# First stage of a two-block kernel: other buffers, PSUM temporaries, another order of the products, keys turned on GpSimd

## What is computed

```python
h = x @ w_in                      # 512 columns for S5, then q, k, v, gate
y_s5 = rms_norm(s5_mixer(u, ...)) # complex diagonal state space, 32 groups, 64 states
q, k = rotary(q), rotary(k)       # 4 heads, 64 wide
out = intra + cross               # retention in chunks, decayed state
out = (out - mu) * rsqrt(var + eps) * gn_gain
y = concat([y_s5, out * silu(gate)]) @ w_out
```

## Time and profile before

| | us |
|---|---|
| median of 3 runs (lowest, highest) | 3410.55 (3409.85, 3413.95) |
| profiled execution, its span | 3408.32, 3406.2 |
| PE busy, share of the span | 3110.5, 91% |
| VectorE, ScalarE, GpSimd busy | 1263.8, 880.2, 990.4 |
| first stage, up to the start of "x1" | 399 |

### The profile page before, as it was taken

How to read it: one execution, slowest core, us unless ns; L and a number is a source line. 1 busy time by engine, 2 the same in 40 slices (tenths; PEclk the granted TensorE clock), 3 DMA queues, 4 the chain that set the end, 5 groups by cost and what they waited for, 6 DMA issues and landing times.

```text
span 3406.2 us, 35503 instructions
## 1 busy us (share of the span) xinstructions
PE 3110.5 (91%) x14706; PEld 2549.1 (75%) x14706; DVE 1263.8 (37%) x2407; ACT 880.2 (26%) x1265; POOL 990.4 (29%) x450
## 2 busy tenths in 40 slices
PE   8688899999999979878997887899999999999995
PEld 7566688888888866656776776788887788888884
DVE  7937751221211254464454444302213311111115
ACT  3212232122121133333334444212111411111111
POOL 5301145232233251101332222122222633333332
PEclk9789999999999989988999999899999999999998
DMA  7323212111111111101110000212112111111111
GB/s 179 81 66 114 105 50 62 50 44 62 50 44 56 48 59 63 37 32 32 38 41 35 32 29 28 81 50 73 46 50 99 49 51 60 46 50 50 50 31 50
DMA packets 67392, 193.18 MB, mean 57 GB/s; under 512 B 10304, under 2 KB 18896, under 8 KB 67216
## 3 DMA queue, kind: packets, MB, share of 16 engines
q1 hardware_dynamic: 67232, 190.91, 18.0%
HBM read 165.46 MB, written 25.43 MB: 56 GB/s over the span
## 4 chain that ended last, share of the span: by engine, by line
PE 79%; DVE 10%; ACT 4%; issue 3%; POOL 3%; DMA 1%; SPq 0%; POOLq 0%; DVEq 0%; ACTq 0%
PE PS L365 45%; PE PS L398 7%; PE PS L399 7%; PE PS L400 7%; PE PS L622 3%; PE PS L862 2%; PE PS L751 1%; POOL WL L2134 1%; DVE s L1423 1%; DVE M L1423 1%; PE PS L481 1%; PE PS L421 1%; POOL DD L2260 1%; PE PS L662 1%; PE PS L779 1%
## 5 line engine op out<-in xcount | busy, mean ns | idle before, releaser
L2134 POOL TENSOR_TENSOR WL<-WR,WH 128x1024 fp32r<-128x1024 f32 x241 | 576.6, 2399 | 2167.7 <-ACT WH L960 2167.6
L365 PE MATMUL PS<-XH,WH 128*128 128x512 f32 x2176 | 692.2, 400 | 11.7 <-DVE XL L1462 9.0
L365 PE MATMUL PS<-XL,WH 128*128 128x512 f32 x2176 | 678.9, 393 | 0.0
L365 PE MATMUL PS<-XH,WL 128*128 128x512 f32 x2176 | 675.3, 392 | 0.0
L365 PEld LDWEIGHTS PS<-XH,WH 128*128 128x128 f32 x2176 | 405.5, 191 | 100.5 <-issue 17.8
L365 PEld LDWEIGHTS PS<-XL,WH 128*128 128x128 f32 x2176 | 414.4, 190 | 88.5
L365 PEld LDWEIGHTS PS<-XH,WL 128*128 128x128 f32 x2176 | 412.7, 190 | 88.1
L960 ACT ACTIVATE WH<-WR 128x1024 fp32r<-128x1024 f32 x241 | 253.1, 1055 | 790.2 <-PE PS L400 481.7
L398 PE MATMUL PS<-WH,HH 128*128 128x512 f32 x864 | 338.9, 392 | 14.4 <-POOL HL L2166 14.4
L399 PE MATMUL PS<-WL,HH 128*128 128x512 f32 x864 | 338.1, 391 | 0.0
L400 PE MATMUL PS<-WH,HL 128*128 128x512 f32 x864 | 337.8, 391 | 0.0
(11 more groups left out here) (314 smaller groups left out, 3820.8 us busy)
## 6 DMA issues: line engine op xcount, KB each, us to landing
WR<-in_weights SPq DMA_DIRECT2D x241, 512.0 KB, 3.6
spill<-STQ SPq DMA_DIRECT2D x24, 256.0 KB, 2.0
BR<-brbuf SPq DMA_DIRECT2D x12, 512.0 KB, 4.4
RAWX<-in_xT SPq DMA_DIRECT2D x8, 512.0 KB, 7.1
RES<-in_x SPq DMA_DIRECT2D x8, 512.0 KB, 6.8
xbuf<-XF SPq DMA_DIRECT2D x8, 512.0 KB, 2.7
brbuf<-STG SPq DMA_DIRECT2D x8, 512.0 KB, 2.7
RES<-xbuf SPq DMA_DIRECT2D x8, 512.0 KB, 7.3
```

The lines of the kernel that those rows point to most:

```text
L365: last = e.matmul(PS[:, u.b + h, :], w, x[:, k, 512 * h:512 * h + 512], start=k == 0 and w is w1 and x is xh, stop=k == nk - 1 and w is w2)
L2134: e.tensor_tensor(WL[:, v % NSPL, :], WR[:, v % NRAW, :], WH[:, v % NSPL, :].bitcast(F), ALU.subtract).then_inc(w_lo, 1)
```

## The change

It puts the retention's buffers elsewhere and issues its first loads at the fourth `s_ss`; holds two PSUM banks ("prep") for temporaries and copies in `dve_in`, until the ET table is done; calls for the sines one product earlier; orders kernels, injections, v steps and outputs anew; turns the keys on GpSimd; applies the norm on ScalarE and the gain where the output is cut (C_GN, a column table, takes the place of GNG); and counts `done` without gaps. The new semaphore `r_st` says that the statistics are ready. `pool_keys(i)` has the seven products of `keys(i)` on GpSimd, with its waits.

```diff
--- before.py
+++ after.py
@@ Units.through @@
-        self.done += 1
+        while self.done in self.gone:
+            self.done += 1
 
 
@@ tiles (QKC to YR were 172 to 203, GNG is gone) @@
+        QKC = sb("QKC", 148, [128, 2, 512])
+        KQT = sb("KQT", 152, [128, 2, 4, 128])
+        QX = sb("QX", 156, [128, 2, 2, 128])
+        PT = sb("PT", 158, [128, 2, 4, 128])
+        TA = [sb("TA0", 162, [128, 8, 32]), sb("TA1", 221.25, [128, 8, 32])]
+        KZ = [sb(f"KZ{k}", at, [128, 256]) for k, at in enumerate((202, 203, 163))]
+        YR = sb("YR", 198, [128, 2, 512])
+        VVC = sb("VVC", 164, [128, 3, 512])
+        GGC = sb("GGC", 170, [128, 2, 512])
...
@@ tiles @@
-        KTS = [sb("KTS0", 198, [16, 8, 128]), sb("KTS1", 142, [16, 8, 128])]
+        KTS = [sb("KTS0", 198, [16, 8, 128]), sb("KTS1", 208, [16, 8, 128])]
-        GL = sb("GL", 148, [128, 4, 1024], R)
-        SG = sb("SG", 164, [128, 2, 1024])
+        GL = sb("GL", 182, [128, 4, 1024], R)
+        SG = sb("SG", 174, [128, 2, 1024])
@@ pe_mixer, at its start @@
+            prep = claim(e, "prep", 2, hold=True, told=False)
@@ pe_mixer @@
             values = pe_token_steps(e, "v", "w_in", 1024, 0, 8, XH, XL, range(8))
+            bk.let(prep)
             kernel_of(0)
             inject(0)
             inject(1)
             kernel_of(1)
+            inject(2)
+            inject(3)
+            kernel_of(2)
             tick(values, 1)
-            kernel_of(2)
             kernel_of(3)
-            for q in range(2, 8, 2):
-                inject(q)
-                inject(q + 1)
-                if q < 6:
-                    tick(values, 1)
-            for q in range(4):
-                outputs(q)
-                if q < 3:
-                    tick(values, 1)
+            inject(4)
+            inject(5)
+            tick(values, 1)
+            inject(6)
+            inject(7)
+            tick(values, 1)
+            outputs(0)
+            outputs(1)
+            tick(values, 1)
+            outputs(2)
+            tick(values, 1)
+            outputs(3)
@@ act_in @@
-                if p == 2:
+                if p == 1:
@@ act_s5, kernel_of @@
-                elif p:
-                    e.wait_ge(s_et, 1)
@@ act_retention @@
             for n in range(12):
+                if 3 <= n < 11:
+                    i = n - 3
+                    u = lots["ro", i]
+                    e.wait_ge(r_st, i + 1)
+                    if i >= 2:
+                        e.wait_ge(lots["rt", i - 2].full, lots["rt", i - 2].nfull)
+                    for h in range(4):
+                        c = slice(128 * h, 128 * h + 128)
+                        t = e.activation(YR[:, i % 2, c], PS[:, u.b, c], ACT.Identity, bias=s6[:, 44 + h:45 + h],
+                                         scale=s6[:, 36 + h:37 + h])
+                    t.then_inc(u.drained, 1)
...
-                    e.activation(XH[:, 4:8, 128 * i:128 * i + 128], four(u), ACT.Copy).then_inc(r_hi, 1)
+                    for j in range(4):
+                        t = e.activation(XH[:, 4 + j, 128 * i:128 * i + 128], PS[:, u.b, 128 * j:128 * j + 128], ACT.Copy,
+                                         scale=cols[:, C_GN + j:C_GN + j + 1])
+                    t.then_inc(r_hi, 1)
                 if n == 0:
-                    act_spill(e, "v", 6)
-                    act_spill(e, "v", 7)
+                    for i in (5, 6, 7):
+                        act_spill(e, "v", i)
@@ dve_in @@
+            prep = lots["prep"]
+            near = PS[:, prep.b, 0:256].rearrange("p (a b c) -> p a b c", a=2, b=8)
+            turn = PS[:, prep.b, 256:288]
+            far = PS[:, prep.b + 1, :]
+            e.tensor_copy(near, PP[:, :, 0:8, :]).then_inc(dve, cv.up())
...
             def pw(ri, gg):
-                return PP[:, ri, 0:8, gg].rearrange("p t (g o) -> p g t o", o=1).to_broadcast([128, 4, 8, 16])
+                return near[:, ri, :, gg].rearrange("p t (g o) -> p g t o", o=1).to_broadcast([128, 4, 8, 16])
...
+            m1, m2 = far.rearrange("p (g c) -> p g c", g=4), M2[:, :, :]
                 then(e.tensor_tensor, split(m1), wide(bR), pw(0, gg), ALU.mult)
-                then(e.tensor_tensor, split(m2), wide(bI), pw(1, gg), ALU.mult)
+                e.tensor_tensor(split(m2), wide(bI), pw(1, gg), ALU.mult).then_inc(dve, cv.up())
                 then(e.tensor_tensor, BB[:, gg, 0, :], m1, m2, ALU.subtract)
                 then(e.tensor_tensor, split(m1), wide(bI), pw(0, gg), ALU.mult)
-                then(e.tensor_tensor, split(m2), wide(bR), pw(1, gg), ALU.mult)
+                e.tensor_tensor(split(m2), wide(bR), pw(1, gg), ALU.mult).then_inc(dve, cv.up())
                 e.wait_ge(dve, cv.n)
                 e.tensor_tensor(BB[:, gg, 1, :], m1, m2, ALU.add).then_inc(s_bb, 1)
...
-                v1, v2 = (x.rearrange("p a b -> p (a b)")[:, 0:gn * m].rearrange("p (g c) -> p g c", c=m)
-                          for x in (E1[:, :, :], E2[:, :, :]))
+                v1 = far[:, 0:gn * m].rearrange("p (g c) -> p g c", c=m)
+                v2 = E1[:, :, :].rearrange("p a b -> p (a b)")[:, 0:gn * m].rearrange("p (g c) -> p g c", c=m)
+                then(e.tensor_copy, turn, LL[:, 8:10, :].rearrange("p a b -> p (a b)"))
                 for g in range(0, 16, gn):
-                    bm = lambda x: x[:, g:g + gn].rearrange("p (g o) -> p g o", o=1).to_broadcast([128, gn, m])
-                    cmul(ET[:, g:g + gn, 0, m:2 * m], ET[:, g:g + gn, 1, m:2 * m], ET[:, g:g + gn, 0, 0:m],
-                         ET[:, g:g + gn, 1, 0:m], bm(P1), bm(P0), v1, v2)
+                    bm = lambda k: turn[:, 16 * k + g:16 * k + g + gn].rearrange("p (g o) -> p g o", o=1).to_broadcast([128, gn, m])
+                    aR, aI = ET[:, g:g + gn, 0, 0:m], ET[:, g:g + gn, 1, 0:m]
+                    then(e.tensor_tensor, v1, aR, bm(1), ALU.mult)
+                    e.tensor_tensor(v2, aI, bm(0), ALU.mult).then_inc(dve, cv.up())
+                    then(e.tensor_tensor, ET[:, g:g + gn, 0, m:2 * m], v1, v2, ALU.subtract)
+                    then(e.tensor_tensor, v1, aR, bm(0), ALU.mult)
+                    e.tensor_tensor(v2, aI, bm(1), ALU.mult).then_inc(dve, cv.up())
+                    then(e.tensor_tensor, ET[:, g:g + gn, 1, m:2 * m], v1, v2, ALU.add)
                 m *= 2
                 if m < 128:
                     squared()
             e.wait_ge(dve, cv.n)
             e.tensor_copy(LAM[:, :], LL[:, 7, :]).then_inc(s_et, 1)
+            e.tensor_copy(E2[:, 0, 0:1], far[:, 0:1]).then_inc(prep.drained, 1)
@@ dve_retention, norm, and its order of work @@
-                if i >= 2:
-                    e.wait_ge(lots["rt", i - 2].full, lots["rt", i - 2].nfull)
-                for h in range(4):
-                    c = slice(128 * h, 128 * h + 128)
-                    t = e.scalar_tensor_tensor(YR[:, d, c], PS[:, u.b, c], s6[:, 24 + 2 * h:25 + 2 * h], GNG[:, c],
-                                               ALU.subtract, ALU.mult)
-                    t.then_inc(u.drained, 1) if h == 3 else t.then_inc(dve, cv.up())
+                e.scalar_tensor_tensor(s6[:, 44:48], s6[:, 24:32:2], -1.0, s6[:, 36:40], ALU.mult, ALU.mult).then_inc(r_st, 1)
+
+            def gated(i):
+                d, u = i % 2, lots["ro", i]
-                for h in range(4):
-                    c = slice(128 * h, 128 * h + 128)
-                    t = e.scalar_tensor_tensor(YR[:, d, c], YR[:, d, c], s6[:, 36 + h:37 + h], GGC[:, d, c], ALU.mult, ALU.mult)
-                    t.then_inc(r_y, 1) if h == 3 else t.then_inc(dve, cv.up())
+                e.tensor_tensor(YR[:, d, :], YR[:, d, :], GGC[:, d, :], ALU.mult).then_inc(r_y, 1)
...
-                if n < 8:
-                    keys(n)
+                if 3 <= n < 11:
+                    gated(n - 3)
-                    e.tensor_tensor(XL[:, 4:8, 128 * i:128 * i + 128], four(u), XH[:, 4:8, 128 * i:128 * i + 128].bitcast(F),
-                                    ALU.subtract).then_inc(u.drained, 1)
+                    for j in range(4):
+                        w = slice(128 * i, 128 * i + 128)
+                        t = e.scalar_tensor_tensor(XL[:, 4 + j, w], PS[:, u.b, 128 * j:128 * j + 128], cols[:, C_GN + j:C_GN + j + 1],
+                                                   XH[:, 4 + j, w].bitcast(F), ALU.mult, ALU.subtract)
+                    t.then_inc(u.drained, 1)
@@ gpsimd: pool_keys, new (the seven products of keys(i) as before, on GpSimd), and its call @@
+        def pool_keys(e, i):
...
+            e.wait_ge(qk_in[i % 2], 16 * (i // 2 + 1))
...
+            if i >= 3:
+                e.wait_ge(lots["kv", i - 3].full, lots["kv", i - 3].nfull)
...
-            pool_cut(e, lots["v", 7].units)
+            for i in range(8):
+                if i == 2:
+                    pool_cut(e, lots["v", 7].units)
+                pool_keys(e, i)
@@ sp_s5 and sp_retention @@
             load(e, lots["qk", 7].units)
```

(36 more changed lines are left out.)

71 lines of the change are left out of this document (32 added, 39 removed).

## The result

The changed kernel takes 3432.32 us (median of 4 runs, 3431.33 to 3433.58), the kernel before, run beside it, 3411.65 (3409.85 to 3413.95). The ratio is 1.006, with a 95% interval from 1.0043 to 1.0078: 20.7 us slower. The forecast was 3396, in a range from 3374 to 3411. The profiled execution has a span of 3429.5 us against 3406.2; squares(3) ends at 422.8 instead of 399.4, and that is the whole difference, 23.4 us in these two executions: behind it the traces run alike.

What follows compares the result with a forecast made beforehand. It took VectorE's chain from sines to first turned injection as the bound; first flip at 221 plus retention 164 ends at 385 instead of 399.4, so 3408.3 - 14.4 = 3393.9, or 3396 against the median; range 3374 to 3411 us.

Steps and rivals of the forecast that it cites:

- the head to T: Preparation up to T, the end of ET: T at 119 us instead of 144.0, within 103 to 130.
- one with an input in PSUM does not take turns: Preparation: VectorE operations with a PSUM input run unhindered beside GpSimd; BB's operations 0.72 us each, ending at 71.7.
- Rival D: BB and ET: PSUM does not lift turn-taking, T at 136 to 141; 3419 us from T = 137; chance 0.08.
- from T to the first flip: Stretch from the end of ET to the retention's start: 102.2 us, first flip at 221 instead of 240.9.
- the first output then takes 15.1 us, the others 8.4: Outputs behind PE's stand for T8: only the first runs at PEclk 0.50; with two v steps 52 us.
- the retention: First flip to the end of squares(3): 164 us against 158.5 before, ends 152 and 172.
- Rival C: Retention: GpSimd's rotations and VectorE's norms take turns every step, 172 us or more; 3404 to 3413 us; chance 0.17.
- With one v step moved in, 124: Retention: PE's products alone take 118 us, 124 with the moved v step.
- n = 5, stall 10: Retention, outs(3) waiting for the ro bank, low parts and norm(2): PE stalls 10 us instead of 6.4.
- n = 6 to 8, "3 us, as 3.2 before": Retention, steps 6 to 8: PE stands 3 us, as 3.2 before.
- The mended counter takes the idle 10.05 away: Retention's tail: ScalarE's idle 10.05 us at 364 goes; only 3 us of the tail go, 11 instead of 14.
- Low clock 5: Retention: 5 us added to the sum of 164 for PE's low clock.

Runs made afterwards that it cites:

- e12: Changed kernel with the temporaries of the state-space preparation back in SBUF, orders and waits as changed; 3451.6 us.
- e6: e2 plus, in SyncE's queue, the YP loads behind the first turn's weight loads and the load of QKC's chunk 2 ahead of them; 3417.3 us.
- e2: Changed kernel with one value step moved back ahead of the first output; 3425.7 us.
- e3: Changed kernel with ScalarE's four scaled copies that drain the ro bank issued ahead of the sigmoid of the turn before; 3424.7 us.
- e9: Changed kernel with the norm applied on VectorE by four operations right behind its statistics, ScalarE's copies dropped; 3416.4 us.
- e7: Changed kernel with ScalarE cutting the GLU's second weight unit ahead of the last gate step's eviction; 3428.8 us.
- e16: e11 with three value steps ahead of the first output and one between first and second, none behind; 3374.9 us.
- e8: Changed kernel with the keys' rotation back on VectorE instead of GpSimd; 3427.5 us.
- e13: e11 with one thing changed back, the keys' rotation on GpSimd; 3397.3 us.
- e11: Changed kernel with the edits of e6 and e7, and keys and norm back on VectorE; 3393.4 us.
- e10: Changed kernel with the edits of e2, e3, e6 and e7 together, keys left on GpSimd and norm on ScalarE; 3407.9 us.
- e14: e11 with one value step moved from behind the second output to between first and second; 3382.9 us.

## Why the prediction was wrong

**Right: the head to T.** VectorE went on behind the sines at 40.5 (41.4 forecast), BB ended at 70.4 (71.7), the squarings took 11.4 us (15), and ET ended at 115.2 (119, within 103 to 130). The step "one with an input in PSUM does not take turns", read off, is shown by e12, also for products that write to PSUM beside it. PE waited at kernel 0 until T, as said. Rival D falls. The 62 cycles more that the Trainium skill (VectorE: DVE Perf Modes, the section on the TRN2 errata) has for an input in PSUM do not show: 512 elements take 0.68 to 0.69 us with one (62.93 in the changed kernel) or without (56.20 in e12).

**Mis-sized: from T to the first flip, 102.2 forecast, 111.7 measured.** T8 landed at T + 51.1 (49.5) and PE stood 8.1 us (8). The step that failed is "the first output then takes 15.1 us, the others 8.4": the second took 14.9, 6.5 more, and the value step behind it 7.7 instead of 5.7. The earlier trace rows showed an output at 0.50 and one at 1.00, and I read the recovery as coming with the first output; it came with the value step that lay between them and that the change moves away. So the head gained 14.0 us, not 20.

**Wrong: the retention, 164 forecast, 195.9 measured.** The sum had 35 us of standing and 129 of work; measured were 53.8 and 142.1. The time lies above every rival, C's 3404 to 3413 included. By its terms:
- *"With one v step moved in, 124"* counted the step as 5.6 us of PE and nothing else. What I left out is what it issues besides: an eviction into a queue of two slots and a store on SyncE, now behind twelve transfers of ybuf and YP. Weight waits were put at "3, as before"; they were 10.2 at the gate step and 4.1 at glu(2). This is the first of the two steps that failed most: the moved step was costed as work alone. e6, which has the edit of e2 in it, gives 15.0 us back.
- *n = 2, stall 8*: 8.0. *n = 5, stall 10*: 8.6.
- *n = 6 to 8, "3 us, as 3.2 before"*: 10.0. This is the second. I had costed ScalarE's four copies by duration (1.2; measured 1.5) and not by what they stand behind: twice the sigmoid, with the bank of `ro` drained by the engine that waits for PE (2.65 us each). The third wait, 4.72, is the 3.19 of before grown, and stays in e3 (4.75) and e9 (4.40). A wait of 2.46 at flip 4 had no term. e3 gives 7.6 back, e9, which takes the copies off ScalarE, 16.0.
- *"The mended counter takes the idle 10.05 away"* had the sign wrong: behind that idle time stood the early cut of the GLU's second unit (364.24), and without it PE stood 4.1 us for this unit. e7 shows 3.5, within what the runs can't tell apart. From there to the end of squares(3) PE stood 14.4 us (4.12, 2.22, 5.43, 2.67), before 9.0 (1.71, 5.50, 1.81).
- *Low clock 5*: the work took 142.1 against 124, so 18. The term was too small from the start: the earlier trace rows have 130.2 of work where the sum has 118, and the sum's own terms for the kernel before (118, 5.6, 6.4, 3.2, 3, 14) make 150.2 of its 158.5 us, so 8 to 12 us of low clock were there already. I have no run that separates the rest; where the stands are mended it is less (127.0 of work in e16, which has one value step fewer there).

**Rival C** had the right sign at the retention and named the wrong cause. Its price, over 8 us for turn-taking, measured 4 to 5 (e8, e13), neither of them clear of the spread.

In the balance: the head gains 14 us on the changed kernel's own path, and the five parts that e11 undoes or mends cost 39. What is left open is how those 39 split. The intervals of e2, e3, e7 and e8 overlap with the changed kernel's, so their single figures are estimates; e6 (15.0), e9 (16.0), e10 and e11 are clear of it.

## What to carry to other kernels

Cost a moved step by everything it issues, and find for each piece what stands ahead of it in its new queue; a buffer of two slots makes the store of step n part of step n + 2. An engine that drains a bank must not have, ahead of the drain, an instruction that waits for the engine which wants the bank: the copies took 1.5 us a chunk, their place behind the sigmoid cost some 7.6 in all, and having them on ScalarE 16.0. And where a part gains and the whole loses, run the parts alone and then mend the others together: here the single parts account for what the joint run gained, to within a few microseconds. The new head with its queues in order is 0.5% faster than the kernel before (e11), and 1.1% with the value steps placed so that PE never stands for T8 (e16), where the whole change was 0.6% slower.

## What the runs showed of the hardware

- A stand of 2.3 us of PE was followed, some 1 us into the output behind it, by a granted clock of 0.50 to that output's end (e14), one of 1.8 us likewise (e6), and without a stand the same products ran at 1.00 (e16). Once low, it stayed at 0.50 through two outputs (tiles of 128x128), 29.9 us with PE busy all the time; the next value step (products of 128x512) ran at 0.73 and what followed at 1.00.
- A VectorE product with one of its two inputs in PSUM takes 0.69 us for 512 elements beside GpSimd's, as one wholly in SBUF does alone, wherever its output goes, and GpSimd's keep their 1.23 and 1.45; 16 elements with both inputs in SBUF take up to 1.30 beside GpSimd (71.08 in the changed kernel) against 0.17 (104.62).
- Where VectorE and GpSimd take turns, a small shift decides which operations meet: ET ended at 115.2 in one execution and at 119.9 in another with the same preparation, by weight cuts that came 6.4 us earlier.
